# Inverse roots of all norms as exp(-ln/2) on ScalarE, in a twelve-layer kernel on one core

## What is computed

```python
def rms_norm(x, g):                       # ahead of each layer: over 1024 values; in dsa and
    xf = x.astype(jnp.float32)            # multi also over the 64 values of each q and k head
    y = xf * lax.rsqrt(jnp.mean(xf * xf, axis=-1, keepdims=True) + RMS_EPS)
    return (y * g.astype(jnp.float32)).astype(x.dtype)

# rwkv: the key norm, a recurrence over the 256 tokens, and a norm over each head behind it
    kk = kk * lax.rsqrt(jnp.maximum(jnp.sum(kk * kk, axis=-1, keepdims=True), 1e-24))
...
    mu = jnp.mean(y, axis=-1, keepdims=True)
    var = jnp.mean(jnp.square(y - mu), axis=-1, keepdims=True)
    y = ((y - mu) * lax.rsqrt(var + RW_GN_EPS)).reshape(B, S, D) * ln_w + ln_b

# stick-breaking attention: log_sigmoid in place of a softmax
        log_1m = jnp.where(earlier, jax.nn.log_sigmoid(-z), 0.0)
        between = lax.cumsum(log_1m, axis=3, reverse=True) - log_1m
        att = jnp.where(earlier, jnp.exp(jax.nn.log_sigmoid(z) + between), 0.0)

# multi: three kinds of attention (4, 6 and 6 heads), each output normed for itself
    mix = jnp.concatenate([rms_norm_2(out_a, og[:NA_W]), rms_norm_2(out_d, og[NA_W:NA_W + DIL_W]),
                           rms_norm_2(out_c, og[NA_W + DIL_W:])], axis=-1)
    return x + mix @ w_out_l
```

## Time and profile before

| | |
|---|---|
| median of three runs | 2569.04 us (2568.66 to 2577.06) |
| the profiled execution | 2572.77 us, of it the span 2571.0 |
| TensorE busy | 2367.9 us (92%) |
| VectorE busy | 1713.2 us (67%) |
| ScalarE busy | 1174.1 us (46%) |
| GpSimd busy | 199.5 us (8%) |
| reciprocals of layer norms, L1804 | 12 of 1751 ns |
| reciprocals of output norms, L2092 | 6 of 1748 ns |
| mean granted clock of TensorE | 0.947 |

### The profile page before, as it was taken

One profiled execution on the slowest core, in us unless ns is written; L12 is line 12 of the kernel. 1 busy time (PEld: TensorE's weight loads), 2 busy tenths in 40 slices (PEclk: granted clock), 3 DMA queues, 4 the chain that ended last, 5 costly groups with the idle time before them and its releaser, 6 DMA issues.

```text
span 2571.0 us, 55843 instructions
## 1 busy us (share of the span) xinstructions
PE 2367.9 (92%) x22886; PEld 2208.8 (86%) x22886; DVE 1713.2 (67%) x2432; ACT 1174.1 (46%) x1936; POOL 199.5 (8%) x249
## 2 busy tenths in 40 slices
PE   6799799998899997999978997999988999988999
PEld 5689799997899996699966897999966999966998
DVE  6744576564656698665576545665876777876776
ACT  5433344446644453554454333444545444545443
POOL 1000010010100131100010000000221000221000
PEclk8789899999999998999987998999989999998999
DMA  4220155541455441255422202654422564413553
GB/s 168 90 84 4 43 197 179 188 139 58 145 189 181 143 134 61 90 180 191 148 70 91 84 4 63 209 176 159 148 66 94 177 196 161 143 50 101 182 183 123
DMA packets 88434, 327.16 MB, mean 127 GB/s; under 512 B 9808, under 2 KB 9936, under 8 KB 87632
## 3 DMA queue, kind: packets, MB, share of 16 engines
q1 hardware_dynamic: 87984, 322.72, 38.0%
q0 software_dynamic: 288, 2.10, 0.2%
HBM read 323.73 MB, written 1.05 MB: 126 GB/s over the span
## 4 chain that ended last, share of the span: by engine, by line
PE 72%; DVE 18%; ACT 4%; issue 4%; POOL 1%; DMA 0%; DVEq 0%; ACTq 0%; SPq 0%; POOLq 0%
PE bank L1232 14%; PE bank L1233 14%; PE bank L1234 14%; PE bank L1254 4%; PE bank L1255 4%; PE bank L1256 4%; DVE w_split L1792 4%; DVE work L1979 3%; ACT w_split L1526 2%; PE bank L491 2%; PE bank L1422 2%; PE bank L1401 1%; PE bank L500 1%; DVE h_split L1822 1%; PE bank L514 1%
## 5 line engine op out<-in xcount | busy, mean ns | idle before, releaser
L1232 PE MATMUL bank<-h_split,w_split 128*128 128x256 f32 x3168 | 919.3, 290 | 38.3 <-DVE h_split L1822 24.0
L1233 PE MATMUL bank<-h_split,w_split 128*128 128x256 f32 x3168 | 904.3, 285 | 0.0
L1234 PE MATMUL bank<-h_split,w_split 128*128 128x256 f32 x3168 | 903.0, 285 | 0.0
L1792 DVE TENSOR_TENSOR w_split<-ring_a,w_split 128x1024 fp32r<-128x1024 f32 x468 | 572.9, 1250 | 183.4 <-ACT w_split L1526 181.4
L1232 PEld LDWEIGHTS bank<-h_split,w_split 128*128 128x128 f32 x3168 | 610.4, 193 | 55.1 <-DVE h_split L1822 33.4
L1233 PEld LDWEIGHTS bank<-h_split,w_split 128*128 128x128 f32 x3168 | 605.4, 191 | 2.1
L1234 PEld LDWEIGHTS bank<-h_split,w_split 128*128 128x128 f32 x3168 | 604.9, 191 | 0.0
L1526 ACT ACTIVATE w_split<-ring_a 128x1024 fp32r<-128x1024 f32 x468 | 476.8, 1050 | 131.1 <-PE bank L1234 115.4
L1254 PE MATMUL bank<-act_split,d_split 128*128 128x256 f32 x1008 | 285.1, 283 | 2.4 <-DVE act_last L1871 2.4
L1255 PE MATMUL bank<-act_split,d_split 128*128 128x256 f32 x1008 | 285.1, 283 | 0.0
L1256 PE MATMUL bank<-act_split,d_split 128*128 128x256 f32 x1008 | 285.0, 283 | 0.0
(11 more groups left out here) (290 smaller groups left out, 3461.3 us busy)
## 6 DMA issues: line engine op xcount, KB each, us to landing
ring_a<-wa SPq DMA_DIRECT2D x474, 512.0 KB, 4.4
ring_d<-wd SPq DMA_DIRECT2D x132, 512.0 KB, 4.3
tab_sb<-tab SPq DMA_DIRECT2D x1, 2448.0 KB, 13.4
planes<-na POOLq DMA_DIRECT2D x2, 1024.0 KB, 6.4
xT<-x SPq DMA_DIRECT2D x1, 1024.0 KB, 4.9
out<-xT SPq DMA_DIRECT2D x1, 1024.0 KB, 3.9
vec_sb<-vec SPq DMA_DIRECT2D x1, 288.0 KB, 4.9
tab_sb<-tab SPq DMA_DIRECT2D x1, 65.0 KB, 4.6
```

What stands on the lines that cost most here:

```text
L1232: mm(dst, w[:, 0, ks], x[:, 0, k, :], start=(k == 0), stop=False)
L1233: mm(dst, w[:, 0, ks], x[:, 1, k, :], start=False, stop=False)
L1234: last = mm(dst, w[:, 1, ks], x[:, 0, k, :], start=False, stop=(k == KT - 1))
L1792: v.tensor_tensor(w_split[:, u % 4, 1, :], ring_a[:, u % 4, :], w_split[:, u % 4, 0, :].bitcast(f32), ALU.subtract).then_inc(s["w_lo"], 1)
```

## The change

Every Sqrt but the key norm's (L702) becomes two instructions of ScalarE, Ln of the same operand and Exp of -0.5 times the result; every reciprocal of a root on VectorE is deleted, with the steps that waited for it. The Exp is what now signals the semaphore that the Sqrt signalled. `root_table` no longer takes a root but loads one set of tables by name, which holds Ln, Exp and simple functions such as Square and Copy; the rwkv part calls it too, ahead of its norm.

```diff
@@ rwkv, ScalarE
             def deviation(c):
                 act.wait_ge(s["gn_var"], 4 * r + c + 1)
-                A(gn_t, eight(chain_bank(c, "y")[:, :]), ACT.Sqrt, bias=T("gn_eps")).then_inc(s["gn_std"], 1)
+                inverse_root(gn_t, eight(chain_bank(c, "y")[:, :]), T("gn_eps"), 1.0, s["gn_std"])
...
             for i in range(12):
                 tokens(i)
-            A(small[:, 63:64], T("eps"), ACT.Sqrt)
+            root_table()
@@ rwkv, VectorE
-            def inverse(c, h):
+            def normed(c, h0, h1):
                 dve.wait_ge(s["gn_std"], 4 * r + c + 1)
-                t = gn_t[:, 4 * h:4 * h + 4, :]
-                step.did(v.reciprocal(t, t))
-
-            def normed(c, h0, h1):
                 step.settle()
...
-            inverse(2, 0)
-            inverse(2, 1)
             normed(2, 0, 2)
             centre(3)
             o_low_of(2)
             low(32)
             gained(3)
-            inverse(3, 0)
             normed(3, 0, 1)
-            inverse(3, 1)
             normed(3, 1, 2)
@@ ScalarE
             def root_table():
-                A(small[:, 63:64], T("eps"), ACT.Sqrt)
+                nc.scalar.preload_act_table_set("natural_log_exp_and_others")
+
+            def inverse_root(dst, src, bias, scale, sem):
+                step.did(A(dst, src, ACT.Ln, bias=bias, scale=scale))
+                step.settle()
+                A(dst, dst, ACT.Exp, scale=-0.5).then_inc(sem, 1)
...
             def norm_rope_std(L, n):
                 act.wait_ge(s["nr_mm"], L["tiles"] + n + 1)
-                A(root_(n), B[n % 4][:, 0:S], ACT.Sqrt, bias=T("eps")).then_inc(s["nr_std"], 1)
+                inverse_root(root_(n), B[n % 4][:, 0:S], T("eps"), 1.0, s["nr_std"])
@@ VectorE
             def rms_inverse(L):
                 dve.wait_ge(s["std_ready"], L["part"] + 1)
-                step.did(v.reciprocal(inv_rms(), inv_rms()))
-                step.settle()
...
                 if gained:
                     dve.wait_ge(s["nr_std"], L["heads"] + n + 1)
-                    step.did(v.reciprocal(r, r))
...
                 def normed_segment(seg):
                     dve.wait_ge(s["on_std"], 3 * r + seg + 1)
-                    step.did(v.reciprocal(work[:, 3 + seg, :], work[:, seg, :]))
                     for n in range(*SEGMENTS[seg]):
                         dve.wait_ge(s["ot_evac"], L["pairs"] + n + 1)
-                        step.settle()
```

More of the change, by code:

```diff
@@ L667, in rwkv_pe, with rwkv_act @@
             out_proj(L, 30, rw_o_split, skipped=3)
-        def rwkv_act(act, L, A, hi):
+        def rwkv_act(act, L, A, hi, root_table, inverse_root):
             u, r, j = L["u"], L["rw"], L["idx"]
@@ L1105, in rwkv_dve @@
             gained(0)
-            inverse(0, 0)
             factor(3, 3)
-            inverse(0, 1)
             carry(1)
@@ L1117, in rwkv_dve @@
             low(30)
-            inverse(1, 0)
             factor(3, 5)
-            inverse(1, 1)
             normed(1, 0, 2)
@@ L1557, in root @@
                 act.wait_ge(s["ssum_ready"], L["part"] + 1)
-                A(inv_rms(), norm_bank(L["part"])[:, 0:S], ACT.Sqrt, bias=T("eps"), scale=1.0 / D)\
-                    .then_inc(s["std_ready"], 1)
+                inverse_root(inv_rms(), norm_bank(L["part"])[:, 0:S], T("eps"), 1.0 / D, s["std_ready"])
             def ffn(L):
@@ L1766, in out_root @@
                 act.wait_ge(s["on_sum"], 3 * L["multis"] + seg + 1)
-                A(work[:, seg, :], B[6 + seg % 2][:, S:2 * S], ACT.Sqrt, bias=T("eps"),
-                  scale=1.0 / ((b - a) * P)).then_inc(s["on_std"], 1)
+                inverse_root(work[:, seg, :], B[6 + seg % 2][:, S:2 * S], T("eps"), 1.0 / ((b - a) * P), s["on_std"])
             for L in plan:
@@ L1774, in _ @@
                 dict(ffn=ffn, stick=stick, dsa=dsa, multi=multi,
-                     rwkv=lambda L: rwkv_act(act, L, A, hi))[L["kind"]](L)
+                     rwkv=lambda L: rwkv_act(act, L, A, hi, root_table, inverse_root))[L["kind"]](L)
         @block.vector
@@ L2091, in normed_segment @@
                     dve.wait_ge(s["on_std"], 3 * r + seg + 1)
-                    step.did(v.reciprocal(work[:, 3 + seg, :], work[:, seg, :]))
                     for n in range(*SEGMENTS[seg]):
                         dve.wait_ge(s["ot_evac"], L["pairs"] + n + 1)
-                        step.settle()
                         v.scalar_tensor_tensor(out=oT[:, n, :], in0=oT[:, n, :], scalar=V(f"out_g{L['idx']}", n),
-                                               in1=work[:, 3 + seg, :], op0=ALU.mult, op1=ALU.mult)\
+                                               in1=work[:, seg, :], op0=ALU.mult, op1=ALU.mult)\
                             .then_inc(s["on_ready"], 1)
```

## The result

| | before | after |
|---|---|---|
| median | 2569.94 us (2568.66 to 2577.06, 4 runs) | 2531.70 us (2530.52 to 2532.96, 4 runs) |
| ratio | | 0.9842, 95% interval 0.9827 to 0.9857 |
| profiled execution, its span | 2572.77, 2571.0 us | 2532.53, 2530.8 us |
| VectorE busy | 1713.2 us | 1579.6 us |
| ScalarE busy | 1174.1 us | 1192.0 us |

The kernel became faster by 38.2 us, 1.5% by the medians and 1.6% by the ratio. Ahead of the result 39.9 us had been worked out, and 2529 us for the time. VectorE lost 134 us of work, and less than a third of it came off the time.

The account below looks back on a forecast made before the run. TensorE, busy for all 76 us of a multi layer's projections, was taken as the bound, so gains lay only in its waits. The terms summed to 39.9 us off the 2569.04 median: 2529 us, own range 2520 to 2541 (71%).

Parts of the forecast that it names:

- (a): End of the recurrence, two rwkv layers: shorter TensorE waits without reciprocals, 5.7 us each, 11.4 gained.
- (b): End of the projections, two multi layers: VectorE no longer behind, less half clock; 7.0 us each, 14.0 gained.
- (c): Output norms of multi, two layers: a table load and three reciprocals go, three Exps come; 10.4 us gained.
- (d): Stick: table loads leave the paths TensorE waits on, and some half clock may go; 5.0 us gained.
- (e): Norms ahead of the rwkv layers: 1.3 us gained in the second, 0.4 in the first, 1.7 in all.
- (f): The kept Sqrt of the rwkv layers needs a new table load on a serial path; 2.6 us lost for two.
- (g): Projections of dsa and multi, ffn starts and first-use tables: covered by other work, so nothing gained or lost.
- The handover as a rival: In the projections TensorE would wait for VectorE, itself waiting for Ln and Exp: 2556 to 2582 us 4%, over 2582 2%.
- The rule against the row: The Trainium skill's 1.38 us drain per table-set switch, absent from the trace; with it the sum gives 2526 us.
- The clock as a rival: Half-clock stretches behind shrinking waits: more vanish, 2505 to 2520 us, 12%; they stay and another comes, 2541 to 2556, 9%.
- the rival of the chain: The projections' 48 reciprocals come off the time in full, 80 us, with the rest 2455 us; chance 1%.
- The signs: Profile marks of being right: multi's transpose wait about 0.5 us, rwkv's product wait 3 to 4, 30 loads, unchanged projection stages.

Follow-up runs that it names:

- back_qk: The changed kernel with the 48 reciprocals of the query and key norms put back on VectorE; 2547.45 us (ratio 0.9910 to the kernel before).
- fill_qk_12: back_qk with 12 filler matmuls of constants, whose result nobody reads, ahead of TensorE's transposes in each multi layer; 2541.06 us (0.9888).
- back_out: The changed kernel with the six reciprocals of multi's output norms put back on VectorE; 2541.89 us (0.9890).
- stick_loads: The changed kernel with eight table loads put back into stick, where the kernel before had them; 2537.93 us (0.9861).
- back_gn: The changed kernel with the 16 reciprocals of the norm behind the recurrence put back on VectorE; 2543.81 us (0.9903).
- kk_ln: The changed kernel with the kept Sqrt of the key norms made Ln and Exp too; 2528.12 us (0.9822).
- two_loads: The changed kernel with two table loads added ahead of the last root behind the recurrence, in both rwkv layers; 2535.49 us (0.9860).
- fill_tail: The changed kernel with filler matmuls ahead of output products: 12 in each multi layer, 6 and 16 in each rwkv layer; 2529.97 us (0.9826).

## Why the prediction was right, point by point

- **What bounds the kernel.** Right, by the stage of after (76.00 of 76.00 us) and by back_qk: 15.8 us for 48 reciprocals, where the chain had promised 75 to 84.
- **(a) the recurrence.** Forecast 11.4, the lead shows 9.5. The two waits came down by 2.55 and 2.91, 5.46 in a layer, which is the sum's 5.2 without the clock. Mis-sized was the rest: the product L595 was hoped to keep the full clock, for up to 1.0; it gained 0.3 in the first layer (1.79 us where it had taken 2.08) and nothing in the second. And the output product behind it ran at half longer than in before, which took 1.0 back in the first layer and 0.6, net, in the second.
- **(b) the projections.** Forecast 14.0, the lead shows 15.9 for the two multi layers (back_qk's 15.8 holds dsa's share too). The wait fell by 4.73, as worked out. The step on the clock behind it was the right one: 3.1 us as far as the first L1400 (fill_qk_12 shows that they are the clock's). In the loop of the attention 1.6 more came in the first layer, and 1.2 were lost in the second. At the end of dsa's projections the lead rose by 1.4, and 1.1 of it went again at half the clock right behind.
- **(c) the output norms.** Forecast 10.4, the lead 9.7. The waits came down by 3.42 and 1.13 in the first layer, by 2.80 and 1.33 in the second, and 0.53 in each at the sums ahead of them: 5.1 and 4.7, forecast 5.2 each.
- **(d) stick.** Forecast 5.0, the lead 6.6. The wait of 3.21 fell to 1.11, by 2.10 (forecast 1.96), and its three long waits together by 4.4 (forecast 4.2). The clock was mis-sized: the suffix sums ran at full speed and gave 4.0, the output product stayed at half longer and took 1.5 back; the sum had 0.8 for it.
- **(e) the norms.** The second layer gave 1.34 of wait (forecast 1.3). The first gave nothing (forecast 0.4): its wait was 13.52 before and 13.60 after, and the whole began 1.0 us later. The prediction had no term for the first table load. In before it ran while ScalarE still waited for its data, in after it stands behind that wait and ahead of the squares that TensorE needs. The first load in before, then in after:

```profile
0.75 1.28 ACT L1530 ACT_TABLE_LOAD   x1 [0.75 <-PEq L2368]
...
6.56 1.28 ACT L1518 ACT_TABLE_LOAD   x1 [6.56 <-DMA vec_sb<-vec]
7.85 2.56 ACT L1537 ACTIVATE sq<-xT 128x256 f32<-128x256 f32 x8
```

  TensorE's first matmul came at 7.37 in before and 8.41 in after, and at 8.40 to 8.80 in every trace with the changed `root_table`. Naming the set by hand had this price, and no run tried the load ahead of the wait.
- **(f) the kept Sqrt.** Forecast -2.6, the lead fell by 1.42 at each, -2.8. The load shows as forecast, and nothing stands around it:

```profile
59.20 1.28 ACT L702 ACT_TABLE_LOAD   x1
60.49 0.60 ACT L702 ACTIVATE work<-bank 128x512 f32<-128x512 f32 x1
61.11 1.28 ACT L704 ACT_TABLE_LOAD   x1
...
64.77 0.76 PE L386 MATMUL bank<-work,ring_a 64*128 64x256 f32 x1 [3.94 <-DVE h_split L894]
```

  2.52 became 3.94. The product behind these matmuls then reached the full clock sooner and gave 0.9 back in each layer; that is in the rows "rest of the rwkv", for which nothing was forecast.
- **(g) the rest.** Forecast nothing, the lead lost 2.6 in ffn, dsa and ffn. No wait of TensorE there grew by more than 0.4, and behind their first products the six ffn layers took the same time to 0.03 us in both traces; the lead falls over neighbouring matmuls, where TensorE runs at half the clock. The same stretch in traces of kernels that have after's code there: back_out lost 2.6 too, stick_loads, back_gn and kk_ln gained 1.2 to 1.6, two_loads and fill_tail 4.7. So this was the chance of single executions, and it is worth up to 7 us between two traces of the same code.
- **The handover as a rival** did not appear: 593 matmuls in 76 us with 21 us of work less on VectorE, and no idle time of TensorE in them.
- **The rule against the row** fell, in its own term and in two_loads. The forecast without it was 2529, with it 2526.
- **The clock as a rival** had been weighed for size only. That it was a lever of its own, some 8 to 10 us, had not been seen.
- **Two slips in the sums**, neither of which moved the forecast: the high end of (d) enters as 8 where 4.2 and 3 make 7.2, and the rival of the chain comes to 2463 and not 2455 (2569 less 80 and the 25.9 of the other terms).
- **The signs.** The waits of 0.59 and 3.58, the 30 loads, none of them in stick, and the length of the projections came as said. The two waits in multi came down by 4.5 and 4.1 together, where 5 had been said; the rest of the 5.2 was at the sums ahead of them. The start of the ffn layer behind stick lost 1.6 us in after's trace, over the 1 us that was to count against the prediction; 0.2 at most in those of back_gn, two_loads and kk_ln.

The terms were off by up to 2 us in both directions, the stretch of (g) lost 3.0, and 3.3 came in the rwkv layers and at the end where nothing was forecast. That the sum came within 3 us of the result is in part these cancelling.

## What to carry to other kernels

Look for what a faster instruction gives in the waits of the bounding engine, place by place, not in its share of the chain of waits: here the chain promised 75 us for lines that were worth 16 to 18. Before counting an engine's spare time, see where in the loop it lies; at a balance of two engines a removal gains a fraction of what an addition costs (0.33 against 1.84 us here). And a pause of TensorE has two prices, the wait and the slow matmuls behind it; fillers that fit into the pause, sized from a row of the trace, took away the second where the matmuls behind it did not wait for another engine anyway (2.9 and 3.1 us behind the recurrences, 0.2 and 0.1 in multi's output products).

## What the runs showed of the hardware that was not expected

- The half clock behind a pause was a third or more of what the pause cost: 3.1 us of 8.2 in a multi layer. It went away with fillers in the pause, although the pause itself stayed.
- A filler of 128x256 in plain float32 ran as two passes: 12 were 24 rows, 5.34 us; 36 took 15.70.
- Waits on serial paths were the same to 0.01 us from one kernel to the next (1.44, 3.58 and 2.48 wherever they were left as they are), while whole times of one kernel spread by 2 to 12 us. Traces with the same code between stick and the second rwkv layer differ there by up to 7.3 us, in pieces of 1 to 2 us, at places where the clock is at half in the one and not in the other.
